# Experts' weighted rows: summed on TensorE for every group, or sent row by row to a table in HBM

## The reference, cut to what matters

```python
g_prob, g_sel = lax.top_k(softmax(t @ w_grp + b_grp), 1)
in_grp = take(t @ w_rtr + b_rtr, g_sel)                     # 8 logits of the chosen group
e_prob, e_sel = lax.top_k(softmax(in_grp), 2)
gate = g_prob * e_prob / sum(e_prob)
hid = silu(t @ w1[e]) * (t @ w3[e])                          # width 256
ffn = sum over the 2 experts of (hid * gate) @ w2[e]
h = layer_norm(ALPHA * h + ffn)
```

## Time and profile before

| | us |
|---|---|
| median of three runs | 1532.8 |
| the profiled execution | 1532.48 |
| its span, first to last instruction | 1530.7 |
| TensorE busy | 1434.4 |
| VectorE busy | 573.2 |
| ScalarE busy | 469.8 |
| GpSimd busy | 30.8 |

### The profile page before, as it was taken

How to read it: one execution, slowest core, us unless ns; L and a number is a source line. 1 busy time by engine, 2 the same in 40 slices (tenths; PEclk the granted TensorE clock), 3 DMA queues, 4 the chain that set the end, 5 groups by cost and what they waited for, 6 DMA issues and landing times.

```text
span 1530.7 us, 18283 instructions
## 1 busy us (share of the span) xinstructions
PE 1434.4 (94%) x7146; PEld 916.2 (60%) x7146; DVE 573.2 (37%) x1188; ACT 469.8 (31%) x1037; POOL 30.8 (2%) x34
## 2 busy tenths in 40 slices
PE   4999989999999989989999999898998979999997
PEld 3777567784788867564444433687876654444442
DVE  2234213252586583331212112568575231221113
ACT  3245332362643234212111211463234412121211
POOL 0000000000011000000000000002100000000000
PEclk9999989999999999969999999999999979999999
DMA  8332253322420132229899896231032329999990
GB/s 333 110 110 86 81 198 108 111 100 108 150 87 29 58 136 83 110 110 367 344 387 390 353 412 257 104 110 56 29 138 82 138 110 385 384 393 408 390 421 37
DMA packets 43867, 298.65 MB, mean 195 GB/s; under 512 B 5104, under 2 KB 5616, under 8 KB 10368
## 3 DMA queue, kind: packets, MB, share of 16 engines
q1 hardware_dynamic: 42064, 287.46, 47.9%
q10 hardware_dynamic: 1712, 9.94, 1.8%
HBM read 296.33 MB, written 1.05 MB: 194 GB/s over the span
## 4 chain that ended last, share of the span: by engine, by line
PE 80%; DVE 14%; ACT 4%; issue 1%; DMA 1%; DVEq 0%; ACTq 0%
PE ps L921 21%; PE ps L1527 15%; PE ps L1555 7%; PE ps L1570 4%; PE ps L1595 4%; PE ps L1166 4%; PE ps L955 4%; PE ps L1427 3%; PE ps L1359 1%; PE ps L1368 1%; PE ps L1625 1%; PE ps L1373 1%; DVE projT L2373 1%; DMA few_all<-few 1%; PE ps L1128 1%
## 5 line engine op out<-in xcount | busy, mean ns | idle before, releaser
L921 PE MATMUL ps<-hT,ring 128*128 128x272 f32 (+1 forms) x2016 | 484.3, 396 | 7.7 <-ACT projT L1716 3.1
L921 PEld LDWEIGHTS ps<-hT,ring 128*128 128x128 f32 x2016 | 383.9, 194 | 86.4 <-issue 11.0
L1527 PE MATMUL ps<-ring,arena 128*64 128x512 f32 x672 | 190.0, 599 | 0.0
L2669 DVE TENSOR_TENSOR arena<-arena,ps 128x256 f32<-128x256 f32 x32 | 13.5, 421 | 294.5 <-ACT arena L2070 294.5
L1527 PE MATMUL ps<-projT,arena 128*64 128x512 f32 x352 | 116.6, 598 | 1.1 <-DVE arena L2670 1.1
L1527 PEld LDWEIGHTS ps<-ring,arena 128*64 128x64 f32 x672 | 54.3, 137 | 88.1 <-issue 88.0
L1555 PE MATMUL ps<-ring,arena 128*64 128x512 f32 x336 | 79.4, 592 | 0.0
L1570 PEld LDWEIGHTS ps<-arena 128*128 128x128 f32 x512 | 62.0, 198 | 26.9 <-issue 24.3
L1823 ACT ACTIVATE projT<-ps 128x272 f32<-128x272 f32 x68 | 27.0, 397 | 142.7 <-PE ps L921 141.3
L2053 ACT ACTIVATE arena<-ps 128x512 f32<-128x512 f32 x64 | 38.2, 596 | 105.9 <-PE ps L1570 105.7
L1570 PE MATMUL ps<-arena 128*128 128x128 f32 x512 | 68.2, 288 | 2.4 <-DVE arena L2653 2.4
(11 more groups left out here) (440 smaller groups left out, 1709.4 us busy)
## 6 DMA issues: line engine op xcount, KB each, us to landing
ring<-experts SPq DMA_DIRECT2D x126, 1024.0 KB, 9.0
projT<-experts SPq DMA_DIRECT2D x66, 1024.0 KB, 8.9
ring<-w_in SPq DMA_DIRECT2D x64, 1024.0 KB, 4.9
ring<-w_out SPq DMA_DIRECT2D x16, 1024.0 KB, 4.9
prm<-params ACTq DMA_DIRECT2D x2, 2048.0 KB, 8.1
cst<-consts ACTq DMA_DIRECT2D x1, 2688.0 KB, 10.3
prm<-params ACTq DMA_DIRECT2D x2, 1152.0 KB, 9.2
res<-x SPq DMA_DIRECT2D x1, 1024.0 KB, 7.5
```

What stands on the lines that cost most here:

```text
L921: mm = pe.matmul(ps[:, 5 + j % banks, 0:ncols], w[:, j % 2, k, :], hT[:, k, T - ncols:T], start=(k == 0), stop=(k == KC - 1))
L1527: mm = pe.matmul(ps[64 * e:64 * e + 64, 0, :], xg[:, 4 * h + k, 64 * e:64 * e + 64], w[e][:, 512 * k:512 * k + 512], start=(h == 0 and k = ...
```

## The change

Groups 0 to 2 (12 of the 16 pairs, `SENT`) no longer go through `add_up`, the sum per group and `back`. Instead `slot_codes` multiplies the unweighted `psel` with two columns per expert, its slots' weights and a row code, so that each expert slot (a partition) has its weight and the number of a row in a table in HBM. The table `chosen` has one row of 1024 for each token and rank (first or second expert), 2 x 272 rows. VectorE weights the expert rows as it copies them out of PSUM into one of two buffers `xo`, and GpSimd sends the 128 rows with one indirect DMA per pair; rows of empty slots have a number outside the table and are dropped. After the twelfth send GpSimd waits for all of them and reads the table back, token tile by token tile, and in the third pair of the last group VectorE adds ALPHA times the residual and both rows (`chosen_added`). Group 3 goes the old way, alone; its sums are copied half by VectorE and half by ScalarE. Both tables are zeroed by GpSimd during the first mixer, from a zeroed part of `sg`, and the first gate sigmoid waits for that. Some semaphores of the overflow branch share numbers with others.

```diff
+NO_ROW = 4096
+SENT = EXPERTS // 2 - PER_GROUP // 2
...
+        chosen = [nc.dram_tensor(f"chosen_{l}", (2 * T, D), F32, kind="Internal").ap() for l in range(LAYERS)]
...
+        xy, ax = more(room, D)
+        xselT, ax = more(ax, T)
         xsel, ax = more(ax, 3, P)
         xrows, ax = more(ax, D)
...
+        xplaces, ax = more(ax, 3 * PER_GROUP)
         psel, ax = more(ax, PER_GROUP, EXPERT_SLOTS)
         pselw, ax = more(ax, PER_GROUP, EXPERT_SLOTS)
...
+        pselT, ax = more(ax, PAIRS_A_GROUP, P)
...
-        xo, ax = more(ax, D)
+        xo, ax = more(ax, 2, D)
...
+        slot_rows = posi[:, 0:2 * PAIRS_A_GROUP].rearrange("p (a b) -> p a b", a=2)
+        late_rows, al = more(AR - 4 * D, 2, 2, D)
+        assert ax <= AR - 4 * D
+        chosen_rows = [late_rows[:, 0], hT.rearrange("p k n -> p (k n)")[:, 0:2 * D].rearrange("p (r d) -> p r d", r=2),
+                       late_rows[:, 1]]
...
                 def turn_group(g):
-                    for t in tiles:
-                        n = ROWS[t]
-                        tr = pe.transpose(ps[:, 4, COL[t]:COL[t] + n], xsel[0:n, t, :], ident[0:n, 0:n])
-                    tr.then_inc(s("group_turned"), 1)
+                    if g:
+                        pe.wait_ge(s("pair_rows_copied"), 2 * (PAIRS_A_GROUP * g - 2))
+                    if g == GROUPS - 1:
+                        for t in tiles:
+                            n = ROWS[t]
+                            tr = pe.transpose(ps[:, 4, COL[t]:COL[t] + n], xsel[0:n, t, :], ident[0:n, 0:n])
+                        tr.then_inc(s("group_turned"), 1)
                     if g == 0:
                         pe.wait_ge(s("routing_ready"), 1)
                     for t in tiles:
                         n = ROWS[t]
-                        mm = pe.matmul(ps[:, 5, 0:2 * PER_GROUP], xsel[0:n, t, :],
-                                       lg[0:n, t, 256 + 2 * PER_GROUP * g:256 + 2 * PER_GROUP * (g + 1)],
+                        mm = pe.matmul(ps[:, 5, 0:3 * PER_GROUP], xsel[0:n, t, :],
+                                       lg[0:n, t, 256:352].rearrange("p (w e) -> p w e", w=3)
+                                       [:, :, PER_GROUP * g:PER_GROUP * (g + 1)],
                                        start=(t == t0), stop=(t == 2))
                     mm.then_inc(s("group_places_in"), 1)
...
+                    if i % PAIRS_A_GROUP == 2 and i + 2 < PAIRS:
+                        pe.wait_ge(s("pairs_selected"), i // PAIRS_A_GROUP + 2)
+                    if i == SENT - 2:
                         pe.wait_ge(s("group_turned_copied"), 1)
                         pe.wait_ge(s("pairs_turned_copied"), 1)
-                    if i % PAIRS_A_GROUP == 2:
-
-                        pe.wait_ge(s("group_turned_copied"), i // PAIRS_A_GROUP + 2 if i + 2 < PAIRS else GROUPS)
-                        pe.wait_ge(s("pairs_turned_copied"), i // PAIRS_A_GROUP + 2 if i + 2 < PAIRS else GROUPS)
...
+                def slot_codes(g):
+                    pe.wait_ge(s("pairs_selected"), g + 1)
                     if g:
...
+                        pe.wait_ge(s("slot_codes_read"), g)
+                    both = xplaces[:, PER_GROUP:3 * PER_GROUP].rearrange("p (w e) -> p w e", w=2)
+                    for q in range(PAIRS_A_GROUP):
+                        mm = pe.matmul(ps[:, 6, 4 * q:4 * q + 4], psel[:, 2 * q:2 * q + 2, :],
+                                       both[:, :, 2 * q:2 * q + 2], start=True, stop=True)
...
+                def turn_pairs():
+                    pe.wait_ge(s("pairs_weighed"), 1)
+                    pe.wait_ge(s("pair_rows_copied"), 2 * (SENT - 2))
                     for q in range(PAIRS_A_GROUP):
                         tr = pe.transpose(ps[:, 5, P * q:P * (q + 1)], pselw[:, 2 * q:2 * q + 2, :], ident)
                     tr.then_inc(s("pairs_turned"), 1)
                 def add_up(i):
...
+                    q = i - SENT
                     if q == 0:
...
+                        pe.wait_ge(s("slot_codes_read"), GROUPS - 1)
                     for half in range(2):
                         pe.wait_ge(s("pair_rows_copied"), 2 * i + half + 1)
...
+                        mm = pe.matmul(ps[:, 6 + half, :], pselT[:, q, :], xo[:, i % 2, 512 * half:512 * half + 512],
                                        start=(q == 0), stop=(q == PAIRS_A_GROUP - 1))
...
-                    turn_pairs(0)
                     for i in range(PAIRS):
                         g, q = i // PAIRS_A_GROUP, i % PAIRS_A_GROUP
                         up_half(i, 0)
                         if i:
                             turn(i - 1)
-                        if q == 3 and g + 1 < GROUPS:
-                            turn_pairs(g + 1)
+                        else:
+                            slot_codes(0)
+                        if q == 3 and g + 2 < GROUPS:
+                            slot_codes(g + 1)
+                        elif q == 3 and g + 2 == GROUPS:
+                            turn_pairs()
                         up_half(i, 1)
                         if i:
                             down(i - 1)
                         if i + 1 < PAIRS:
                             gather_pair(i + 1)
-                        if i:
+                        if i > SENT:
                             add_up(i - 1)
                         if q == 2 and g + 1 < GROUPS:
                             gather_group(g + 1)
...
-                    def back(t, groups):
+                    def back(t):
                         for half in range(2):
-                            for g in groups:
-                                mm = pe.matmul(ps[0:ROWS[t], 2 * t + half, :], xselT[:, g, COL[t]:COL[t] + ROWS[t]],
-                                               xy[:, g, 512 * half:512 * half + 512],
-                                               start=(g == 0), stop=(g == GROUPS - 1))
+                            pe.wait_ge(s("group_sums_copied"), half + 1)
...
+                    back(1)
                     if t0 == 0:
...
+                        for q in range(4):
+                            mm = pe.matmul(ps[32 * q:32 * q + META, 0, 0:256], xselT[:, 0:META],
+                                           xy[:, 256 * q:256 * q + 256], start=True, stop=True)
                         mm.then_inc(s("experts_back"), 1)
...
+                    back(2)
...
+                        if l == 0 and step[1] == 0:
+                            a.wait_ge(zeros_out, 16 * LAYERS)
                         sigmoid(a, L, sg[:, step[1], :], projT[:, GATE + step[1], META:T], s("gate_sigmoid_ready"))
...
+                                if g + 2 == GROUPS:
+                                    turned_in()
                         hidden_in(PAIRS - 1)
...
+                        a.wait_ge(s("pair_summed"), 2)
+                        a.wait_ge(s("group_sums_copied"), 1)
+                        a.activation(xy[:, 512:D], ps[:, 7, :], ACT.Copy).then_inc(s("group_sums_copied"), 1)
...
+            V0(v.memset(sg[:, 0, :], 0.0))
...
+                codes = const("row_codes").rearrange("p (t r) -> p t r", r=2)[:, t0:, :]
+                V(v.tensor_tensor(c(320, 32), c(352, 32), bc(codes[:, :, 0], 32, 2), ALU.mult))
+                V(v.scalar_tensor_tensor(out=c(320, 32), in0=c(196, 32), scalar=float(-T), in1=c(320, 32),
+                                         op0=ALU.mult, op1=ALU.add))
...
+                V(v.tensor_tensor(c(288, 32), c(132, 32), c(196, 32), ALU.add))
                 v.wait_ge(s("places_counted"), 1)
...
+                counts = ps[:, 7, 0:96].rearrange("p (t e) -> p t e", t=3)[:, t0:, :]
+                V(v.scalar_tensor_tensor(out=c(256, 32), in0=counts, scalar=1.0, in1=c(352, 32), op0=ALU.add, op1=ALU.mult),
+                  s("routing_ready"))
...
                     v.wait_ge(s("group_places_in"), g + 1)
-                    VP(v.tensor_copy(xplaces, ps[:, 5, 0:2 * PER_GROUP]))
+                    VP(v.tensor_copy(xplaces, ps[:, 5, 0:3 * PER_GROUP]))
                     v.tensor_tensor(psel, bc(const("slots")[:, 0:EXPERT_SLOTS], PER_GROUP, 1),
                                     bc(xplaces[:, 0:PER_GROUP], EXPERT_SLOTS, 2), ALU.is_equal)\
                         .then_inc(s("pairs_selected"), 1)
                     v.wait_ge(s("pairs_selected"), g + 1)
+                    if g < GROUPS - 1:
+                        return
...
+                def slot_codes_in(g):
+                    v.wait_ge(s("slot_codes_done"), g + 1)
+                    found = ps[:, 6, 0:4 * PAIRS_A_GROUP].rearrange("p (q w e) -> p w e q", w=2, e=2)
+                    for e in range(2):
+                        r = slice(64 * e, 64 * e + 64)
+                        VP(v.tensor_copy(slot_weights[r, g % 2], found[r, 0, e]))
+                        VP(v.tensor_scalar(slot_rows[r, g % 2], found[r, 1, e], -1.0, float(NO_ROW), ALU.mult, ALU.add),
+                           s("slot_codes_read") if e else None)
...
```

(49 more changed lines are left out.)

96 lines of the change are left out of this document (34 added, 62 removed).

## The result

The changed kernel takes 1506.48 us (median of 4 runs, 1503.48 to 1509.63) against 1533.2 for the kernel before (1532.13 to 1534.29): ratio 0.9822, 95% interval 0.9803 to 0.9841. The prediction was 1506.0, range 1487 to 1525. The profiled execution took 1504.99 us, span 1503.2, so 27.5 less than the span of before.

The account below looks back on a forecast made before the run. TensorE was taken to bound the kernel, with the weight loads close behind. The terms 18.5 + 11 - 7 + 2.1 + 3.0 - 1 = 26.6 us, taken from 1532.8, gave 1506 us, range 1487 to 1525.

Parts of the forecast that it names:

- What bounds the kernel before: In the expert stages TensorE sets the pace, busy 255.99 of 257 us in layer 0, with DMA at 0.89 and 0.91.
- TensorE's own saving: Expert stages: less TensorE work, mainly 12 `add_up` at 1.81 us, saves 22.8 us in layer 0 and 22.2 in layer 1.
- The weights decide the rest: Expert stages: weight, row and read-back bytes at 415 GB/s limit the saving to 23.3 us in layer 0, 14.0 in layer 1.
- The ledger: The forecast's account of each expert stage by TensorE's work and by bytes moved, 95.1 and 94.9 MB, the later limit counting.
- mixing: Expert stages: TensorE and loads do not cover each other's pauses; 5 us charged in layer 0, 3 in layer 1.
- uneven rows: Sends in both stages: neighbouring filled slots load few DMA engines; 3.5 us per layer taken, from 0 to 11.3.
- The clock: Expert stages: TensorE's waits at a drained ring may drop its clock; 1 us taken, bounds 0 and 6.
- The ends: After the last down-products: overlapped halves and fewer instructions copying back save 2.1 us in layer 0, 3.0 in layer 1.
- At no cost: Zeroing the tables, weighting rows, adding the table and reading it back were all claimed to be covered by other work.
- TensorE's pace as the bound: Rival: in the expert stages weights arrive fast enough and TensorE still bounds; 51.7 us saved at best, 1481; chance 0.15.
- Dear rows: Rival: row sends use few engines or move empty rows, costing 11.3 us instead of 3.5 twice; 1522; chance 0.19.
- A send that outlasts two pairs: Rival: sends over some 26 us stall VectorE and TensorE; 1606 at 36 us; chance 0.13, shared with several costs together.

Follow-up runs that it names:

- half loads: In layer 1, all weight loads after the first nine bring half their columns: 1533.63 us on the kernel before, 1495.49 us on the changed kernel.
- Slots apart: Changed kernel with the first 64 slot numbers in bit-reversed order, so an expert's filled slots are no longer neighbours; 1502.47 us, ratio 0.9773 to 0.9855.

## Why the prediction was right, step by step

The sum was 26.6, and 27.3 came. Term by term:

- **What bounds the kernel before.** TensorE, with the loads close behind: shown by the half loads, which changed nothing before and 12.3 us after.
- **TensorE's own saving: 22.2 us in layer 1, measured 20.3.** The term that was mis-sized is the price of an `add_up`, 1.81 us from one timeline row pair. In the table of steps a plain pair (step 1) fell from 14.67 to 13.02, so one is worth 1.65; twelve are 19.8 instead of 21.7, which is 1.9 less. The partial products were worth 5.15 (step 15: 14.47 became 9.32), as predicted. The rest, -4.6 by the prediction, is -4.6 measured, but by luck: by their rows the slot codes cost 3.0 instead of 3.5 and the gather's waits 2.3 instead of 2.5, and most of that was used up by the opening of the stage, where the granted clock over 6 us was 0.84 with half loads and 0.96 before (4.29 and 3.81 us for the first 16 up-products). These rows of the list of groups for layer 1's stage show it, first before, then after with half loads (count, busy us, mean ns, idle before):

```profile
L1595 PE MATMUL ps<-arena 128*128 128x512 f32 x60 | 28.4, 596 | 0.0
...
L1636 PE MATMUL ps<-arena 128*128 128x512 f32 x12 | 5.3, 592 | 0.0
```

```profile
L1451 PE MATMUL ps<-res,arena 128*128 128x512 f32 x24 | 11.0, 601 | 2.3 <-ACT arena L2083 2.3
...
L1629 PE MATMUL ps<-arena 128*128 128x512 f32 x16 | 8.0, 619 | 0.0
...
L1610 PE MATMUL ps<-arena 128*128 128x4 f32 x24 | 3.0, 247 | 0.0
```

  And the openings, from TensorE's timelines, in the same order:

```profile
1260.14 3.81 PE L1527 MATMUL ps<-ring,arena 128*64 128x512 f32 x16
```

```profile
1247.59 4.29 PE L1555 MATMUL ps<-ring,arena 128*64 128x512 f32 x16
```

- **The weights decide the rest.** Right in kind: layer 0 gained 13.1 and layer 1 8.0, which is their order as forecast. The ledger gave, with mixing and uneven rows and 0.8 before the stage, 15.0 and 7.5; measured with what lies before each stage, 13.2 and 9.2. That the misses of -1.8 and +1.7 cancel in the sum is luck. Of the rows, 1.5 MB were sent in layer 0 and 1.7 in layer 1, where the ledger had 1.67 and 1.57. How the microseconds are lost differs from the working in one point. The ledger lets the stage end when the last load lands. That load is issued at 1465.81, the DMA share is 0.37 from 1476 to 1480 and 0.00 behind it, and the last group of down-products starts at 1483.31, after 13 us in which TensorE waited for no load. The loads cost time earlier, one late load at a time, and most of it where the read-back crosses them. What I had called mixing and charged 3 us in layer 1 was thus not a small correction to a limit at the end, but the mechanism itself; that the sum still came out near is for the most part because both count the same bytes.
- **Uneven rows: 3.5 a layer, not shown.** Single profiles differ by 2.9 and 2.4, of which the scatter of a stage, 2.3, can be nearly all. Empty slots move nothing; a stage with all 128 rows sent is 8.7 us longer than after.
- **The clock: 1 us taken, about 4.2 measured** (bounds 0 and 6), in the two groups of products behind the longest waits. Layer 1's 1.4 of it is part of the 12.3, and helps to explain why waits for loads were less than forecast: 5.1 and 9.6 us against 9 and 15, while TensorE's whole idle time was 8.7 and 13.2.
- **The ends: 2.1 and 3.0, measured 2.0 and 3.0.** Before the stage, 0.8 a layer: 1.2 in layer 1, but 0.1 in layer 0 (24.95 us from the router to the first up-product became 24.88). The traces show where the rest went there: the 12 products of `gather_group` took 9.00 us instead of 8.38 and the 16 of `gather_pair` 3.78 instead of 3.56, at a granted clock of 0.65 and 0.50 against 0.71 and 0.55. Whether that is more than chance was not tried.
- **At no cost:** right for the zeros (issued from 63.6 us on, both landed by 92.5, no wait of ScalarE), for the weighting (0.75 us for 0.69) and for VectorE's additions in pair 14. Not right for the read-back, which I had put there because it lands in time. It does, in 6.7 to 20.7 us; but it costs 6.1 us by what it takes from the loads. Its bytes were in the ledger, so the sum had them.
- **Rivals.** TensorE's pace as the bound: refuted by the waits and by what the half loads freed. Dear rows: uneven rows alone were to cost 11.3, and the sends with all their bytes cost 4.6. A send that outlasts two pairs: 9.2 us at most against some 26. The share of 0.97 or more at 405 to 425 GB/s "from start to end" holds from 1310 to 1440 (422), not for whole stages (397, 395), which have pauses in their first 60 us and a drained queue in their last.

The Trainium skill's 358 GB/s (DMA: Bandwidth & Descriptors, Specifications), weighed and set aside in the prediction, is not met here either: 422 GB/s over 130 us. The same skill (HBM Reference, Specifications (TRN2)) gives that figure to cores whose neighbour streams too and about 425 to a core alone, with which the trace agrees.

**Open.** In the eleven profiles of the changed kernel and its variants, whose TensorE work ahead of the first expert stage is the same, that stage begins anywhere from 682.6 to 691.6 us. This is as wide as the scatter of the totals within one kernel (4 to 12 us) and the reason why stages are compared here; its cause was not looked for. Slots apart are not shown to be faster than after, neither by their time nor by their stages.

## What to carry to other kernels

Where one engine is at 100% and the DMA share is at 0.9, reckon a saving twice, and then ask at which moment the two streams meet: half-width loads on the kernel before and after tell in two runs how much of a saving is TensorE's and how much the transfers take back. Work moved from TensorE to HBM is paid in bytes, here about 2.8 us per MB where the loads already filled the engines (10.6 us for 3.8 MB); its instructions and its latency cost nothing while they are covered, so the way to make it cheaper is to send fewer bytes (half the width gave 12 us), not to send later: a transfer put behind a full queue lands 20 us on and turns what it saved into a tail. Before a microsecond or two of a stage is called an effect, look at how far a stage with unchanged code moves from run to run: here 2.3 us.
